# VectorE takes the weight sums, the token sums' low parts and the product row's low part from GpSimd; the product row gets its own buffer

## The reference, cut to what matters

```
h  = rmsnorm(x, w)                     # (1032, 1024)
u  = h @ w_up                          # (1032, 2 * 2816), float32
u  = u[t-2]*c[0] + u[t-1]*c[1] + u[t]*c[2]      # causal, per column
z  = silu(u[:, first half]) * u[:, second half]
y  = x + z @ w_down
```

## Time and profile before

| | |
|---|---|
| three runs | 2936.16, 2939.25, 2941.25 us, median 2939.25 |
| the profiled execution, own time | 2937.28 us |
| its span, first to last instruction | 2935.6 us, mean granted clock of TensorE 0.958 |
| TensorE busy | 2596.9 us, 88% |
| VectorE busy | 1577.2 us, 54% |
| ScalarE busy | 1202.6 us, 41% |
| GpSimd busy | 891.1 us, 30% |
| first up-projection | about 1115 to 1590 us |
| second up-projection | about 2208 to 2683 us |

### The profile page before, as it was taken

The page is one execution under the profiler, slowest core; times in us unless marked ns, Lnnn a source line. Parts: engine busy times, 40 slices in busy tenths (PEclk is TensorE's granted clock), DMA queues, the critical chain, the costliest instruction groups (busy, mean ns, idle before and its releaser), DMA issues.

```text
span 2935.6 us, 50423 instructions
## 1 busy us (share of the span) xinstructions
PE 2596.9 (88%) x19111; PEld 1913.2 (65%) x19111; DVE 1577.2 (54%) x2441; ACT 1202.6 (41%) x1737; POOL 891.1 (30%) x716
## 2 busy tenths in 40 slices
PE   5888997998887787898999998999987889999997
PEld 2767666655565454777777665666655777776664
DVE  8264554335899648666664214423358665665213
ACT  4564764324777424444443112211124444443111
POOL 0330312323444204556554000011005555563000
PEclk9898998999999898999999999999998999999999
DMA  3222223363000221111113110111121111113111
GB/s 131 78 73 64 69 65 115 116 190 95 1 1 1 88 94 36 50 50 50 50 50 112 65 49 32 48 49 48 51 92 42 50 50 50 50 50 120 50 54 63
DMA packets 118107, 190.32 MB, mean 65 GB/s; under 512 B 17506, under 2 KB 84435, under 8 KB 117587
## 3 DMA queue, kind: packets, MB, share of 16 engines
q1 hardware_dynamic: 97218, 167.81, 17.8%
q0 software_dynamic: 3792, 12.58, 1.3%
q10 hardware_dynamic: 16960, 8.16, 1.0%
HBM read 169.92 MB, written 22.76 MB: 66 GB/s over the span
## 4 chain that ended last, share of the span: by engine, by line
PE 41%; DVE 18%; issue 14%; ACT 8%; POOL 7%; SPq 6%; DMA 6%; DVEq 1%; POOLq 0%; ACTq 0%
PE PS L2137 29%; DMA W<-wk 4%; POOL R L879 4%; PE PS L2585 2%; ACT xT L995 2%; DVE R L1781 2%; SPq L626 2%; SPq L629 2%; PE PS L2117 2%; DVE R L1451 2%; ACT xT L1383 2%; POOL xT L866 2%; PE PS L2170 1%; DVE xT L1924 1%; ACT R L1340 1%
## 5 line engine op out<-in xcount | busy, mean ns | idle before, releaser
L2137 PE MATMUL PS<-hT,R 128*128 128x344 f16 x4104 | 604.6, 310 | 5.5 <-DVE R L571 4.5
L2137 PEld LDWEIGHTS PS<-hT,R 128*128 128x128 f16 x4104 | 401.6, 98 | 205.8 <-DVE R L571 3.4
L2137 PE MATMUL PS<-R 128*128 128x344 f16 x3276 | 478.4, 309 | 6.6 <-DVE xT L1978 6.5
L571 DVE SCALAR_TENSOR_TENSOR R<-W,R 128x1024 f16<-128x1024 f32 (+1 forms) x102 | 145.5, 1427 | 530.2 <-ACT R L565 529.6
L2137 PEld LDWEIGHTS PS<-R 128*128 128x128 f16 x3276 | 320.3, 98 | 164.4 <-issue 7.0
L2585 PE MATMUL PS<-hT,HM 128*128 128x258 f16 x2016 | 258.9, 289 | 111.1 <-DVE HM L1946 111.1
L565 ACT ACTIVATE R<-W 128x1024 f16<-128x1024 f32 (+1 forms) x102 | 117.6, 1154 | 579.1 <-PE PS L2137 539.7
L2585 PE MATMUL PS<-R 128*128 128x258 f16 x3024 | 340.7, 272 | 0.0
L2585 PEld LDWEIGHTS PS<-R 128*128 128x128 f16 x3024 | 292.4, 97 | 41.6
L1924 DVE SCALAR_TENSOR_TENSOR xT<-xT 128x1024 f32<-128x1024 f32 x176 | 230.2, 1308 | 153.4 <-ACT xT L1383 147.5
L2585 PEld LDWEIGHTS PS<-hT,HM 128*128 128x128 f16 x2016 | 203.9, 103 | 159.0 <-DVE HM L1946 99.5
(11 more groups left out here) (330 smaller groups left out, 4066.9 us busy)
## 6 DMA issues: line engine op xcount, KB each, us to landing
W<-wk SPq DMA_DIRECT2D x154, 512.0 KB, 3.5
W<-wdn SPq DMA_DIRECT2D x32, 704.0 KB, 4.0
xT<-cmp_t SPq DMA_DIRECT2D x256, 64.0 KB, 1.8
xT<-x SPq DMA_DIRECT2D x16, 516.0 KB, 7.4
x_kept_in<-xT SPq DMA_DIRECT2D x16, 516.0 KB, 5.0
xT<-x_kept_in SPq DMA_DIRECT2D x16, 516.0 KB, 6.6
o_y<-hT SPq DMA_DIRECT2D x6, 688.0 KB, 3.4
o_win_s<-state_win POOLq DMA_DIRECT2D x1, 4088.0 KB, 24.2
```

Source lines behind the costliest of these rows:

```text
L571: dve.scalar_tensor_tensor(to[:, n, 1, 0:width], W[:, n, 0:width], UNIT, to[:, n, 0, 0:width], ALU.mult, ALU.subtract).then_inc(w_split, 1)
L2137: ins = pe.matmul(wide(u)[:, m, :], weights[half], src[:, other, m * TW:(m + 1) * TW], start=(first and half == other == 0), stop=(last an ...
```

## The change

GpSimd's `sums`, its two token low parts and its `low` go; it keeps `copies`. VectorE gets them as `weight_sums`, `weight_last_sum`, `token_low(2, 2)`, `token_low(3, 0)` and `low_z`. The product row is written to `ZF`, which lies in the last row of `Z2`, except for the last pair. ScalarE's L1383 waits for the product (`zm_here`) instead of the low part, `high` stands before p5's wait, `part_last_sum` behind the tap. In the opening, `low_a(0)` stands right behind the first token sum, and the order of the token sums is 0, 1, 2, 3 instead of 0, 2, 1, 3.

```diff
+        ZF = reg((KF - 1) * TT, TT)
...
-            def ffn_rows(s, norm, tiles, pairs):
-                n0 = s * WP
-
-                def sums(q, i=None):
...
-                    pool.tensor_tensor(SUMS[:, 2], W[:, 1, 0:D // 2], W[:, 1, D // 2:D], ALU.add).then_inc(s1_here, 1)
...
+            def ffn_rows(s, tiles, pairs):
...
                 def body(q, i=None, first=False, last=False):
-                    if not last:
-                        sums(q + 1, i)
                     copies(q, 1, i)
-                    low(q, i)
                     copies(q + 1, 0, i)
...
-                for turn, b in enumerate((0, 2)):
-                    pool.wait_ge(tm_hi, 4 * s + turn + 1)
-                    pool.tensor_tensor(T2P[b][:, :, 1, :], TF[b], T2P[b][:, :, 0, :], ALU.subtract).then_inc(tm_pool, 1)
...
-                    act.wait_ge(tf_here, 12 * s + 3 * (turn + 1))
+                    act.wait_ge(tf_here, 12 * s + (6, 9, 9, 12)[turn])
...
+                    high(q, i)
                     after("p5")
...
-                    high(q, i)
-                    if not last:
                         hold_first(q + 1, i)
                     after("p3")
...
+                    act.wait_ge(c12_here, at(i, 2, n + 1))
+                    act.wait_ge(zm_here, at(i, 2, pairs + p))
+                    act.activation(YF[0], UF[0][:, 2:2 + TT], ACT.Copy, scale=tap(0)).then_inc(yi_here, 1)
                     if not last:
                         part_last_sum(q + 1, i)
-                    act.wait_ge(c12_here, at(i, 2, n + 1))
-                    act.wait_ge(z_here, at(i, 2, 1 + pairs + p))
-                    act.activation(YF[0], UF[0][:, 2:2 + TT], ACT.Copy, scale=tap(0)).then_inc(yi_here, 1)
...
+                def weight_sums(q, i=None):
+                    for half in range(2):
+                        dve.wait_ge(raw_in[half], at(i, 32, 16 * (n0 + q + 1)))
+                    own.up(dve.tensor_tensor(SUMS[:, 2], W[:, 1, 0:D // 2], W[:, 1, D // 2:D], ALU.add))
+                    dve.tensor_tensor(SUMS[:, 1], W[:, 0, 0:D // 2], W[:, 1, 0:D // 2], ALU.subtract)
+                    own.settle()
+                    dve.tensor_tensor(SUMS[:, 0], SUMS[:, 2], W[:, 0, 0:D // 2], ALU.subtract).then_inc(sum_here, 1)
...
+                def low_z(p, i=None, last=False):
+                    row = Z2[:, ds(p if i is None else i * 2 + p, 1), :, :]
+                    dve.wait_ge(zhi_here, at(i, 2, pairs + p + 1))
...
-                    dve.tensor_tensor(YF[0], YF[0], YF[1], ALU.mult).then_inc(zm_here, 1)
+                    dve.tensor_tensor(YF[0] if last else ZF, YF[0], YF[1], ALU.mult).then_inc(zm_here, 1)
...
                         low_a(q + 1, i)
+                        weight_sums(q + 1, i)
                     after("p7")
                     dve.wait_ge(u4_held, at(i, 2, n + 1))
                     dve.wait_ge(st_here, at(i, 4, 2 + tiles + 2 * p))
                     joined(UF[1][:, 2 + HT:2 + TT], 2, HELD[0]).then_inc(c22_here, 1)
+                    if not last:
+                        weight_last_sum(q + 1, i)
+                    low_z(q, i)
```

More of the change, by code:

```diff
@@ L598, in over_pairs @@
             else:
-                with per.turns((WP - 3) // 2, 12) as i:
+                with per.turns((WP - 3) // 2, 14) as i:
                     for q in (1, 2):
@@ L874, in copies @@
                     pool.tensor_copy(FS[:, ds(t, 1), 0, :], UF[n][:, T + 2:T + 2 + NB].unsqueeze(1)).then_inc(st_here, 1)
[L876 to L880, removed]
                 def body(q, i=None, first=False, last=False):
-                    if not last:
-                        sums(q + 1, i)
                     copies(q, 1, i)
-                    low(q, i)
                     copies(q + 1, 0, i)
-                pool.wait_ge(t_here, KD * TN * (norm + 1))
-                pool.wait_ge(x_kept, 16 * KD * (s + 1))
-                sums(0)
-                for turn, b in enumerate((0, 2)):
-                    pool.wait_ge(tm_hi, 4 * s + turn + 1)
-                    pool.tensor_tensor(T2P[b][:, :, 1, :], TF[b], T2P[b][:, :, 0, :], ALU.subtract).then_inc(tm_pool, 1)
                 copies(0, 0)
@@ L897, in ffn_rows @@
                 copies(KF - 1, 1)
-                low(KF - 1)
                 pool.wait_ge(st_here, 2 + tiles + 2 * KF)
@@ L1410, in ffn_up @@
                 silu(KF - 1)
-                high(KF - 1)
+                high(KF - 1, last=True)
             stage_squares("mix_out", 1, 0)
@@ L2020, in ffn_up, with sums @@
                 places = ((0, 688), (516, 344), (172, 860))
-                def sums(turn, b, one, minus):
-                    if turn > 1:
-                        dve.wait_ge(tf_here, 12 * s + (3 if turn == 2 else 9))
+                def sums(b, one, minus):
                     for m, (f, g) in enumerate(places):
@@ L2030, in sums @@
                         dve.tensor_tensor(TF[b][:, :, at_m], block[one], block[minus], ALU.subtract).then_inc(tf_here, 1)
-                sums(0, 0, "12", "11")
-                sums(1, 2, "22", "12")
-                sums(2, 1, "22", "t1")
-                sums(3, 3, "t2", "21")
+                sums(0, "12", "11")
+                low_a(0)
+                dve.wait_ge(tf_here, 12 * s + 3)
+                sums(1, "22", "t1")
                 dve.wait_ge(x_kept, 16 * KD * (s + 1))
+                weight_sums(0)
                 for n in range(2):
@@ L2039, in ffn_up @@
                 own.settle()
+                sums(2, "22", "12")
+                token_low(1, 1)
+                weight_last_sum(0)
                 dve.wait_ge(u_here, s * (2 + KD) + 1)
@@ L2042, in ffn_up @@
                 taps(YF[0], UF[0], old(0), weight(0), y_here)
-                low_a(0)
-                token_low(3, 1)
+                token_low(2, 2)
+                token_low(3, 0)
+                dve.wait_ge(tf_here, 12 * s + 9)
+                sums(3, "t2", "21")
                 low_sums(0)
+                low_last(0)
                 dve.wait_ge(u_here, s * (2 + KD) + 2)
@@ L2048, in ffn_up @@
                 taps(YF[1], UF[1], old(1), weight(1), tg_here)
-                low_last(0)
                 over_pairs(dve, body, own)
-                product(KF - 1)
+                product(KF - 1, last=True)
+                low_z(KF - 1, last=True)
             for k in range(KD):
```

39 lines of the change are left out of this document (17 added, 22 removed).

## The result

The changed kernel takes 2818.27 us (median of four runs, 2815.54 to 2826.67) against 2940.25 for the kernel before, taken beside it: ratio 0.9584, 95% interval 0.9552 to 0.9617. The profiled execution took 2817.94 us, its span 2816.3. The forecast was 2820, faster.

A forecast was written before the change was run, and what follows sets the result against it. TensorE was taken to idle in each pair waiting for VectorE's low_a, delayed by GpSimd; 2 x (50.8 + 7.8 + 1.2) = 119.6 us off 2937.28, plus 2.0, gives 2820 us, range 2808 to 2866.

The forecast's parts named there:

- The pairs: Steady pairs of the up-projections: TensorE's gap closes, period 18.57 us instead of 21.25, giving 50.8 us per layer.
- Term (c): VectorE's load in a pair: 3.7 us added, 16.3 of 18.57 us in all, so the moved work fits.
- Term (d): Moved instructions in VectorE's queue delay nothing urgent; the raw weights' 3.7 us load is hidden behind 6 us of work.
- The slack: In a pair, low_a would end 12.4 us after p3's end, TensorE needing it after 13.25: 0.8 us to spare.
- (a): ScalarE's row start L1383 waits for the product instead of GpSimd's low part, so it starts 2.3 us earlier per pair.
- (b): Without GpSimd arithmetic beside it, low_a in each pair takes 1.2 us instead of 2.29, saving 1.1 us.
- its last rival: Slower, chance 0.03: late weight loads stop VectorE's queue; weights' ring 14.2 us with a 3.7 load, 22.5 with 12; 2969.
- The opening: Before pair 1: undisturbed token sums and new order start pair 1's p1 at 1151.3 instead of 1159.10, 7.8 us per layer.
- the charge for the clock: In the opening, p6 and p5 after 8.6 us of TensorE idleness are charged 2 us for the lower clock.
- The end: Start of the down-projection: the tap ahead of its join moves earlier, 1.2 us per layer, between bounds 0 and 2.3.
- Friction: Rival, chance 0.17: GpSimd's copies hold up VectorE's chain by 2 us, leaving 1.2 us of gap per period, 2866.
- VectorE did not become the bound: Rival, chance 0.04: added work runs at disturbed rates, VectorE takes 19.6 us a pair, 2858.

The follow-up runs named there:

- kernel 3: Changed kernel with the four weight sums back on GpSimd, token low parts and product row's low part staying on VectorE: 2847.38 us, ratio 0.9686.
- kernel 6: Changed kernel with VectorE making the product twice in 21 pairs of each layer, ahead of the low part of the whole weights: 2845.99 us, ratio 0.9687.
- kernel 7: Kernel before the change, with GpSimd's weight sums waiting for the low part of the whole weights of the same pair: 2956.98 us, ratio 1.0047.
- kernel 1: Kernel before the change, with only the product row put in its own buffer; GpSimd keeps sums and low part: 2876.11 us, ratio 0.9781.
- kernel 2: Changed kernel without the own buffer: product written over YF[0], ScalarE's row start waiting for the low part VectorE makes: 2817.09 us, ratio 0.9582.
- kernel 4: Changed kernel with only the product row's low part back on GpSimd, reading the own buffer: 2821.94 us, ratio 0.9595.
- kernel 10: Changed kernel with the opening's first low part of the whole weights moved behind the first row's taps: 2810.36 us, ratio 0.9569.
- kernel 11: Changed kernel with its opening reordered to the order in which TensorE needs things: 2811.19 us, ratio 0.9565.
- the last three versions: Changed kernel with late first low part, with reordered opening, and with that opening's idleness in two pieces: 2810.36, 2811.19 and 2811.95 us.

## Why the prediction was right

**The sum.** 119.6 us forecast; between the profiled executions 119.3 (2937.28 - 2817.94), by the medians 122.0, and by the stages 60.4 and 60.5.

**The pairs.** 18.57 us forecast, 18.55 measured: 19 x (21.24 - 18.55) = 51.2 us in the first layer, 50.8 forecast. Term (c), VectorE's load, 16.3 forecast and 16.0 measured; the moved sums take 0.69 us each, as the row of that size said. Term (d) held: the load lands ahead of the sums. The slack was overestimated somewhat: 0.5 us instead of 0.8, since L1348 starts 0.16 us behind the end of the copy it reads and not at once, and the chain behind is a little longer. Kernel 3 leaves 0.5 (1.08 us more work, 0.61 lost) and so does kernel 6 (1.26 more, 0.72 lost).

**Where the reason was not right.** (a) and (b) were added up as two delays of `low_a`. The sum was safe, as TensorE bounds the period once both are gone. But in the kernel before the period was set by a ring and not by `low_a`: with `low_a` at 1.22 us it was 21.64 (kernel 7). The meeting counted there as longer sums and not as the 1.1 us of `low_a`, and what its end is worth by itself is open. Only once the row starts early (kernel 1) does the chain over `low_a` end last, as the working has it. The sum came out right because the change shortens the ring too; the working looked at the ring only in its last rival, for the kernel after, at 14.2 us. And (a) names the buffer; what makes the row start early is that either the buffer exists (kernel 1) or VectorE makes the low part (kernel 2). The change has both, and one would do: kernels 2 and 4 have one each, and both have the period of 18.55. Reading, the working also has L864 end 1.1 us late; by the rows it is 1.0 (2.25 against 1.27).

**The opening.** 7.8 us forecast, 7.8 measured (7.6 in the second layer); p6 forecast at 1140.3, measured 1140.04; the charge for the clock 2 us, measured 2.5 and 2.9 in the two layers. TensorE's two idle times are 8.26 and 0.68 us, against 8.6 and 1.2. What was missed: that the idle time could stand elsewhere. The token low parts on VectorE were not taken back by themselves, so their share of the 7.8 us is not shown. **The end.** 1.2 forecast, 1.4 and 1.5 measured.

**The rivals.** Friction did not occur: in the pairs GpSimd's copies take 1.05 to 1.26 us behind a busy VectorE, as before (2.2 and 2.3 in the opening), and nobody waits for them. VectorE did not become the bound: it is busy 16.0 us of a period. The load was never late.

## What to carry to other kernels

A wait that shows in every period is not yet its cause: follow the chain back until it closes on itself, and ask what the ring costs without that wait. An engine's share of busy time says little; the same 1.2 us cost nothing behind the instruction that TensorE waits for and 0.72 to 0.79 ahead of it. When an engine leaves a critical chain, its in-order queue leaves too: GpSimd's small copies were late only because they stood behind its sums.

## What the runs showed of the hardware

An instruction of VectorE that meets one of GpSimd is not slowed by a share but set back by what is left of the other: 1.08 us in kernel 3, 1.34 and 1.94 in kernel 4. The exception is the tap of kernel 1, which lost 0.28 us while GpSimd ran on for 0.48.

Idleness of TensorE of 8.26 us ahead of p6 was followed by a granted clock of 0.50 that cost 1.6 to 2.9 us, in executions of the same code. With 5.2 us ahead of p1 the cost was 1.5 and 2.3 in the two layers of kernel 10, and the later 1.6 us of idleness cost none (8.11). 3.7 us cost 1.7 and 1.4 (kernel 11). The length of the idle time alone does not decide: in the kernel before, 2.42 us in the opening were followed by 24 matmuls in 4.41 us, while 2.57 us in a pair were followed by 24 in 2.82.

The part of the program ahead of the stage, the same in all kernels, moved by up to 8 us between them (1114.75 to 1122.68), which is as much as the last three versions gain: differences that small are read from the stage and not from the whole time.
